# Eight distances between the split weights and the streaming operand, on one NeuronCore

## The reference

```python
for i in range(2):                         # first block
    xn = rms_norm(h, attn_norm[i])
    gq, gk, gv, gr, glr, fq, fk, fv, ff = split(xn @ w_in[i])
    o = concat(gated linear attention, forgetting attention)
    h = h + o @ w_out[i]
    h = h + (silu(g) * u) @ w_down[i]      # u, g: causal conv of rms_norm(h) @ w_up[i]
# second block: q, k, v, index queries and keys, conv and gate inputs from rmsnorm(h) @ w_in
h = h + (sigmoid(ga) * y_attn + sigmoid(gb) * y_conv) @ w_out
h = h + (silu(f @ w_gate) * (f @ w_up)) @ w_down
return rmsnorm(h)[:, 16:]
```

## The kernel before, in words

| matmuls | columns | distance, words |
|---|---|---|
| all with 512 columns (down projection of layer 1, nearly all of the second block, the token-major tiles gv, fv, vv) | 512 | 0 |
| token-major gk (L1602); the last tile's halves (L1538) | 256 | 0 |
| seven products, stage 2 | 256 | 16 |
| up projection of layer 0, most of both attentions' projections, dk | 264 | 16 and 8, in turn |
| up projection of layer 1, cu, cc | 260 | 8 and 4, in turn |
| down projection of layer 0, w_out, seven products of stages 0 and 1 | 264, 260 | changes from step to step, since the operand's rows are 528, 264 or 260 words apart |

## Time and profile before

### The profile page before, as it was taken

The page is one execution under the profiler, slowest core; times in us unless marked ns, Lnnn a source line. Parts: engine busy times, 40 slices in busy tenths (PEclk is TensorE's granted clock), DMA queues, the critical chain, the costliest instruction groups (busy, mean ns, idle before and its releaser), DMA issues.

```text
span 2210.1 us, 39479 instructions
## 1 busy us (share of the span) xinstructions
PE 2184.6 (99%) x15711; PEld 2003.0 (91%) x15711; DVE 1424.6 (64%) x2661; ACT 1069.0 (48%) x2027; POOL 149.3 (7%) x245
## 2 busy tenths in 40 slices
PE   9999999999999999999999999999999999999998
PEld 7799999999997899998899889978899888998997
DVE  5356689559744466898398566869444465863664
ACT  5356556347533465555276534223244444652652
POOL 4111011100000011100000010110000000000001
PEclk9999999999999999999999999999999999999999
DMA  6656778775335546664455262777512222543651
GB/s 200 191 148 162 186 187 235 214 228 177 130 95 156 162 114 160 188 185 147 125 174 160 81 191 96 202 202 206 155 68 67 67 95 87 157 159 118 182 174 51
DMA packets 104738, 336.15 MB, mean 152 GB/s; under 512 B 14967, under 2 KB 19037, under 8 KB 102253
## 3 DMA queue, kind: packets, MB, share of 16 engines
q1 hardware_dynamic: 90460, 227.30, 31.3%
q0 software_dynamic: 13376, 105.03, 20.4%
q10 hardware_dynamic: 720, 1.31, 0.2%
HBM read 331.46 MB, written 102.79 MB: 196 GB/s over the span
## 4 chain that ended last, share of the span: by engine, by line
PE 91%; DVE 4%; ACT 2%; issue 1%; POOL 1%; POOLq 0%; ACTq 0%; DVEq 0%
PE G L1486 54%; PE G L1523 17%; PE G L1602 7%; PE X L1523 3%; PE X L1823 1%; DVE wL L2500 1%; PE X L1910 1%; PE X L1775 1%; PE X L1799 1%; ACT wH L1963 1%; PE X L1894 1%; PE X L1879 1%; PE X L1562 1%; PE X L1866 0%; PE X L1729 0%
## 5 line engine op out<-in xcount | busy, mean ns | idle before, releaser
L1963 ACT ACTIVATE wH<-raw 128x512 fp32r<-128x512 f32 (+3 forms) x741 | 491.8, 685 | 434.0 <-PE G L1486 353.7
L2500 DVE TENSOR_TENSOR wL<-raw,wH 128x512 fp32r<-128x512 f32 (+3 forms) x741 | 556.5, 764 | 217.7 <-ACT wH L1963 214.3
L1486 PE MATMUL G<-aH,wH 128*128 128x264 f32 (+3 forms) x1744 | 445.0, 318 | 3.1 <-DVE aL L2513 2.4
L1486 PE MATMUL G<-aH,wL 128*128 128x264 f32 (+3 forms) x1744 | 426.8, 307 | 0.0
L1486 PE MATMUL G<-aL,wH 128*128 128x264 f32 (+3 forms) x1744 | 426.6, 307 | 0.0
L1486 PEld LDWEIGHTS G<-aH,wH 128*128 128x128 f32 (+1 forms) x1744 | 283.3, 188 | 23.1 <-issue 2.8
L1486 PEld LDWEIGHTS G<-aH,wL 128*128 128x128 f32 (+1 forms) x1744 | 281.5, 187 | 16.2
L1486 PEld LDWEIGHTS G<-aL,wH 128*128 128x128 f32 (+1 forms) x1744 | 281.7, 188 | 13.1 <-issue 0.2
L1523 PE MATMUL G<-seven,wH 128*128 128x256 f32 (+2 forms) x1152 | 212.0, 283 | 2.9 <-DVE wL L2500 1.6
L2661 DVE TENSOR_TENSOR hT<-G,hT 128x528 f32<-128x528 f32 (+1 forms) x83 | 58.0, 699 | 199.3 <-PE G L1486 199.1
L1523 PEld LDWEIGHTS G<-seven,wH 128*128 128x128 f32 x1152 | 177.1, 188 | 5.4 <-issue 3.3
(11 more groups left out here) (412 smaller groups left out, 3968.9 us busy)
## 6 DMA issues: line engine op xcount, KB each, us to landing
raw<-weights SPq DMA_DIRECT2D x179, 512.0 KB, 4.0
weight_sums<-weights POOLq DMA_DIRECT2D x72, 704.0 KB, 6.5
raw<-weight_sums SPq DMA_DIRECT2D x192, 256.0 KB, 2.9
raw<-weights SPq DMA_DIRECT2D x145, 256.0 KB, 2.9
raw<-weights SPq DMA_DIRECT2D x48, 704.0 KB, 4.1
weight_sums<-weight_sums POOLq DMA_DIRECT2D x24, 704.0 KB, 4.8
weight_sums<-weights POOLq DMA_DIRECT2D x24, 512.0 KB, 5.2
weight_sums<-weights POOLq DMA_DIRECT2D x24, 448.0 KB, 5.3
```

What stands on the lines that cost most here:

```text
L1486: done = e.matmul(m.pair(i)[0:M, bank, 0:n], a[:, k, 0:M], b[:, kx, lo - t0:lo - t0 + n], start=(k == 0 and c == 0), stop=(k == nk - 1 and ...
L1963: e.activation(m.high(i)[:, c], m.raw(i)[:, c], ACT.Copy).then_inc(s.w_hi, 1)
L2500: e.tensor_tensor(m.low(i)[:, c], m.raw(i)[:, c], m.high(i)[:, c].bitcast(F32), ALU.subtract).then_inc(s.w_lo, 1)
```

## The change

`behind(i)` gives each tile an offset of 0 to 56 words in steps of 8 (32 bytes), and `places()` adds it to the tile's place. Slots for seven products are 576 words apart (a slot's 512 and 64 for the offset), the buffers `wH` and `wL` get 64 words more each, and a tile is taken to fill its own size and not the slot's. Seven-product tiles get 8 times the pair index (plus the half) modulo 8; feed-forward tiles one offset for two tiles, falling by 8; a tile right behind a seven-product tile 0; gk 48, gv 8, fv 24, vv 40; all others one offset for two tiles, falling by 8. `wH` and `wL` grow by 64 words each, so all later tensors move by multiples of 64 words. Since the offset is the same for `wH` and `wL`, `high`, `low`, `mm` and `prod7` stay as they are.

```diff
+BEHIND = 64
+def behind(i):
+
+    role = ROLE[i]
+    if role[0] == "seven":
+        return 8 * ((role[3] + role[2]) % 8)
+    if i and ROLE[i - 1][0] == "seven":
+        return 0
+    if role[0] in ("down", "d2", "up", "u2", "g2"):
+        n = 2 * role[3] + (len(role) > 4 and role[4]) if role[0] == "up" else 2 * role[2] + (role[0] == "g2") if role[0] in ("u2", "g2") else role[-1]
+        return 8 * (7 - n // 2 % 8)
+    if role[0] in TOKEN_MAJOR:
+        return {"gk": 48, "gv": 8, "fv": 24}.get(role[0], 40)
+    return 8 * (7 - i // 2 % 8)
 def places():
-    last, k = [-1] * (NW * WMAX), 0
+    last, k = [-1] * (NW * WMAX + BEHIND), 0
-            at, k, n = 512 * k, (k + 1) % 5, n + n % 2
+            at, k, n = 576 * k + behind(i), (k + 1) % 5, n + n % 2
         else:
-            at, n = WMAX * (n % NW), n + 1
+            at, n = WMAX * (n % NW) + behind(i), n + 1
         place[i] = at
-        size = 512 if role[0] == "seven" else WMAX
+        size = SIZE[i]
-        self.wH = sb("wH", [128, NW * WMAX], F32R)
-        self.wL = sb("wL", [128, NW * WMAX], F32R)
+        self.wH = sb("wH", [128, NW * WMAX + BEHIND], F32R)
+        self.wL = sb("wL", [128, NW * WMAX + BEHIND], F32R)
```

## The result

| | before | after |
|---|---|---|
| median | 2211.07 us | 2228.49 us (2228.03 to 2228.96, 2 runs) |
| profiled execution, its span | 2211.83, 2210.1 us | 2228.03, 2226.3 us |
| ratio, 95% interval | | 1.0084 (1.0066 to 1.0101) |

The two medians of this table alone would give 1.0079. The kernel before, run again beside the first experiments, had a median of 2209.9 us in 19 executions, and against that the change costs 18.6 us, 1.0084.

The account below looks back on a forecast made before the run. PE's matmul stream was taken to bound the kernel (91% of the chain). Surplus changes of -7.7 + 1.5 - 0.6 + 2.2 - 0.4 = -5.0 us gave 2206 us, range 2194 to 2219.

Parts of the forecast that it names:

- Term 1: 512-column matmuls: 2,840 leave distance 0 and their surplus falls from 13.5 to 10.8 ns, -7.7 us.
- 2 ns over today's: Upper bound for the 512-column matmuls: surplus rising 2 ns over the present one, +5.7 us.
- The test row: Layer 1's down projection, 59.88 us for 264 matmuls before, forecast at 59.3 after; the rivals gave 59.9, 58.3 and 60.1.
- C: Rival: distance 0 is good for 512 columns and changing distances disturb a rhythm; +7 us, 2218; chance 0.23.
- B: Rival: leaving distance 0 and changing at each tile puts PE into the fast rhythm; -23 us, 2188; chance 0.12.
- A: Rival: the distance between weights and stream does not matter; no change, 2211 us; chance 0.13.
- D: Rival: DVE's halves slow by over 31% and seven products wait; each further 10% is 2.3 us per 50 us; chance 0.02.
- Stage 2: Its 1,512 seven-product matmuls: mean surplus from 10.1 to 11.1 ns, +1.5 us, bounds -4.0 and +4.5.
- 264 columns: About 2,400 matmuls at a constant pair of distances: surplus from 10.5 to 11.4 ns, +2.2 us.
- gk and the last tile: 258 matmuls leaving distance 0: surplus from 13.1 to 10.8 ns, -0.6 us.
- 260 columns: 3 x 480 matmuls: surplus from 12.1 to 11.8 ns, -0.4 us.
- the down projection of layer 0: Its distances already change by step; the same set in another order, so 0.

Follow-up runs that it names:

- e4: The kernel before with wH and wL both moved by 40 words and the tensors behind them by 64; 2229.35 us, ratio 1.0089.
- e14: The kernel before with the views of wH and wL both starting 60 words in; 2220.27 us.
- e7: The kernel before with all tensors, operands and weights, moved 8 words later together; 2209.51 us, one execution.
- e1: The changed kernel with every offset 0, keeping its slots, buffers and sizes; 2209.96 us, ratio 1.0001 to the kernel before.
- e10: The kernel before with wL meant to move 60 words; paddings were rounded up, so wL moved 64 and everything behind it 72; 2222.36 us.
- e11: The kernel before with offset 8 for one seven-product tile in each half of stage 2, nothing else; 2209.38 us, ratio 0.9995.

## Why the prediction was wrong

**The bound.** Right: PE's stream bounds the kernel, no wait was added, and the time moved by pitch alone.

**Term 1, 512 columns, is the step that failed.** It put 10.8 ns, the middle of rows with 264, 260 and 256 columns, in the place of an unknown 512-column figure. Measured at the new distances: about 19.4 in the moved tiles, +14.5 us and not -7.7. Behind that lay a reading: "A surplus that does not grow with the columns belongs to something that happens once a matmul", from 13.1 at 256 and 13.5 at 512 columns. The runs refute what was built on it, and suggest another reason for the like numbers. In these steady stretches the pitch of a step of three matmuls is a whole multiple of 6.67 ns, 16 periods of 2.4 GHz:

| row | ns a step | multiple of 6.667 |
|---|---|---|
|, 59.88 x264, 512 at 0 | 680.5 | 102 |
| after, 7.56 per tile, 512 at 48 | 687.3 | 103 |
| e4, 53.90 x231, 512 at 40 | 700.0 | 105 |
|, 8.16 x72, 256 | 340.0 | 51 |
|, 8.48 x72, 256 | 353.3 | 53 |
|, 5.75 x48, 256 at 0 | 359.4 | 54 |

In the trace before, 2,465 of 2,889 sequences of three matmuls with 512 columns (overlapping ones counted, those with a wait left out) take 102 such units (680 ns) within 1 ns, and none is under 679 ns; with everything at distance 40 (e4) it is 105 in 2,403 of 2,894. It is not a law for every stretch. In e4 stage 2, at distance 56, takes 8.40/24 = 350.0 ns a step, 52.5 units, and the gauge of e14 60.28/88 = 685.0 ns, 102.75:

```profile
2057.61 8.40 PE G L1525 x72
```

```profile
1034.63 60.28 PE G L1486 x264
```

The columns alone need 96 and 48. So 13.1 and 13.5 are both two units a matmul, and the alikeness may be that of a scale with few marks; the runs do not prove it. What they do show is that it said nothing of what another distance costs at another length: distance 0 is the slow one with 256 columns (54 units against 51 to 53) and the fast one with 512 (102 against 103 to 105).

**Its range.** The upper bound, "2 ns over today's", had no row; the ends should have come from what was not known, since no 512-column matmul lay at any other distance. The rows with 256 columns alone spread over 6.5 ns (113.3 to 119.8); that spread on 2,840 matmuls would have bounded this term by +18.5 us, and the range would have held the time.

**The test row.** It was to decide between 59.3, 59.9, 58.3 and 60.1, and 61.10 is above them all. It was the right row to look at: it shows that the price is at 512 columns.

**The rivals.** C had the sign and the place (distance 0 is the good one for 512 columns), with 0.23 where I gave the forecast 0.50. Its price of 0.9 ns was that of changing against constant distances at 264 columns; measured it is some 6, and e4 shows that constancy does not help. B's fast rhythm was seen only at 256 columns. A is refuted by e4 against e7: the same program with only the weights moved costs 20 us, with all moved nothing. D is out; DVE's halves kept their 688 ns:

```profile
L2517 DVE TENSOR_TENSOR wL<-raw,wH 128x512 fp32r<-128x512 f32 x616 | 414.4, 688 | 167.2 <-ACT wH L1980 164.2
```

**The rule behind rival A.** 512 columns take 226.7 ns at distance 0 and 233.3 at 40, with the same instructions at the same clock. So the Trainium skill's statement, in "TensorE: Matmul & The Clock Gate", section "What happens when you issue a matmul", that the weight load takes no read bandwidth from the running matmul does not carry over to a time that is blind to the addresses: here their places matter to 3%. The runs don't show whether a port, a bank or the order of loads is the reason. The N/2.4 + 2.5 ns back to back that the Trainium skill gives on that page, under "Wait — 56ns, not 53.3ns?", isn't reached by any steady stretch here; the lowest are 6.7 ns at 256 and 13.3 at 512 columns.

**The small terms.** Stage 2 lost the fast rhythm (+2.6 for +1.5, within its bounds). Against e1, whose stage 2 stands at 12.6 us and not 14.8, it is +4.8, a little over its upper bound of 4.5. 264 columns (+2.0 for +2.2), gk and the last tile (-0.9 for -0.6) and 260 columns (-0.1 for -0.4) came out near what was worked out. For 264 columns that is in part luck: the long piece at 286.80 pays 0.74/576 = 1.3 ns where 0.9 was reckoned, the others less, and the down projection of layer 0, put at nothing, 0.17 us. The analogy within one column count, or between 256, 260 and 264, held in the main; the one across a factor of two did not.

**What stays open.** Why 0 is good, 60 good or nearly so and 62 bad, why 48 and the mixture of 0 and 60 have two rhythms each, and why one bad matmul lengthens its step, were not settled; the runs show that it is so. Nor can they tell whether a weight load is disturbed by the matmul that it belongs to or by the one that streams beside it, since both stream from the same residue. Operands moved against fixed weights were tried only through e10's rounding, with the same result.

## What to carry to other kernels

In this kernel, where every matmul loads its own weights, the place of the weights against the streaming operand modulo 256 bytes is worth 3% of a 512-column float32r matmul. Look at it as a layout choice with a measured table, and not as something to spread evenly: putting the tiles at eight distances gave them the average of seven bad ones and a good one. A class of instructions with a single measured setting has no lower and upper row; bound it by the whole spread that another class shows (6.5 ns here), upwards as well as downwards, and test one tile of it before changing all.

## What the runs showed that I had not expected

- In many long stretches steps of three matmuls keep to whole multiples of 6.67 ns (102, 103 or 105 for 512 columns, 51, 53 or 54 for 256, each from the rows above), with exceptions at 52.5 and 102.75.
- 8 bytes decide: 52.37 us for 231 matmuls at distance 60, 61.60 for 264 at 62.
- One of three matmuls at distance 40 costs as much as all three (61.59 and 61.62 us for 264), while one of three at 60 costs nothing (59.86) there and 4.5 ns a matmul in most up and gate tiles.
- The same program takes different rhythms from run to run and after waits: e11's runs fall at 2208 and at 2209.5 us, and stage 2 had 8.5 to 9.9 ns in four traces with the same distances. A difference of 2 us between two versions can be that alone.
